# Two neighbouring rows per partition: wider expert-weight loads, an early second matrix, and a last norm in partition groups

## The reference

```python
x = _layernorm(DEEPNORM_ALPHA * x + mix, ln1_g, ln1_b)
# per token: top 4 of 32 experts, softmax over the selected logits
hgu = xb @ moe_w_gu[e] + moe_b_gu[e]          # (1024) x (1024, 2048)
gate, up = hgu[:, :D_EXPERT], hgu[:, D_EXPERT:]
gate = jnp.minimum(gate, 7.0); up = jnp.clip(up, -7.0, 7.0)
act = (up + 1.0) * gate * jax.nn.sigmoid(1.702 * gate)
out = act @ moe_w_down[e] + moe_b_down[e]     # (1024) x (1024, 1024)
y = sum over a token's experts of weight * out
x = _layernorm(DEEPNORM_ALPHA * x + y, ln2_g, ln2_b)
```

## Time and profile before

| | |
|---|---|
| median of three timed runs | 1255.13 us |
| the profiled execution | 1250.65 us, span 1248.7 us |
| TensorE busy | 1167.9 us (94%) |
| VectorE, ScalarE, GpSimd busy | 385.5, 278.4, 19.3 us |
| moved by DMA | 456.94 MB, mean 366 GB/s |
| loads of the first matrix from SyncE into `gu_w` | 252 of 1024 KB, and 4 early |
| loads of the second matrix | 256 of 512 KB |

### The profile page before, as it was taken

The page is one execution under the profiler, slowest core; times in us unless marked ns, Lnnn a source line. Parts: engine busy times, 40 slices in busy tenths (PEclk is TensorE's granted clock), DMA queues, the critical chain, the costliest instruction groups (busy, mean ns, idle before and its releaser), DMA issues.

```text
span 1248.7 us, 17368 instructions
## 1 busy us (share of the span) xinstructions
PE 1167.9 (94%) x6686; PEld 643.9 (52%) x6686; DVE 385.5 (31%) x719; ACT 278.4 (22%) x505; POOL 19.3 (2%) x39
## 2 busy tenths in 40 slices
PE   9999999999999999999999997999999999898995
PEld 8999879985434343444344442444343434343441
DVE  4888587753020202122203110211202020202025
ACT  5685454432111010101010110011111101010101
POOL 1000021000000000000000000000000000000000
PEclk9999999999999999998999998999999999999998
DMA  9745578887999999999999999999999999999994
GB/s 281 236 134 172 167 239 271 327 313 289 357 418 416 418 417 418 418 418 418 416 417 418 418 417 416 418 417 418 418 419 417 419 417 419 417 418 418 417 417 160
DMA packets 118351, 456.94 MB, mean 366 GB/s; under 512 B 10408, under 2 KB 49336, under 8 KB 85312
## 3 DMA queue, kind: packets, MB, share of 16 engines
q1 hardware_dynamic: 115728, 447.08, 90.3%
q0 software_dynamic: 2576, 9.21, 2.3%
HBM read 450.30 MB, written 5.95 MB: 365 GB/s over the span
## 4 chain that ended last, share of the span: by engine, by line
PE 73%; DMA 9%; SPq 7%; DVE 4%; issue 3%; ACT 2%; DVEq 0%; ACTq 0%
PE pool L957 25%; PE pool L878 15%; DMA gu_w<-in_moe_w_gu 8%; PE ub L838 6%; PE pool L607 5%; PE pool L608 4%; PE pool L609 4%; SPq L404 4%; PE ob L968 3%; SPq L399 3%; PE ub L968 2%; DMA dn_w<-in_w_in 1%; ACT arena L1204 1%; PE pool L894 1%; PE ob L907 1%
## 5 line engine op out<-in xcount | busy, mean ns | idle before, releaser
L957 PE MATMUL pool<-gu_w,arena 128*64 128x512 f32 x1920 | 425.2, 598 | 6.9 <-DMA gu_w<-in_moe_w_gu 6.9
L957 PEld LDWEIGHTS pool<-gu_w,arena 128*64 128x64 f32 x1920 | 138.4, 138 | 276.9 <-issue 247.2
L878 PE MATMUL pool<-dn_w,arena 128*64 128x512 f32 x1024 | 226.7, 595 | 20.3 <-ACT arena L1204 20.3
L1682 DVE TENSOR_SCALAR arena<-pool 128x512 f32<-128x512 f32 x31 | 21.4, 692 | 713.0 <-PE pool L957 708.1
L607 PE MATMUL pool<-xh,wh 128*128 128x264 f32 x568 | 164.4, 289 | 1.3 <-DVE xl L1254 0.6
L609 PE MATMUL pool<-xh,wl 128*128 128x264 f32 x568 | 161.4, 284 | 0.0
L878 PEld LDWEIGHTS pool<-dn_w,arena 128*64 128x64 f32 x1024 | 70.8, 137 | 156.0 <-issue 128.5
L1199 ACT ACTIVATE arena<-arena 128x512 f32<-128x512 f32 x32 | 20.2, 630 | 471.3 <-DVE arena L1682 471.3
L607 PEld LDWEIGHTS pool<-xh,wh 128*128 128x128 f32 x568 | 107.7, 190 | 8.0 <-issue 4.1
L608 PE MATMUL pool<-xl_most,wh 128*128 128x264 f32 x385 | 110.0, 286 | 0.0
L609 PEld LDWEIGHTS pool<-xh,wl 128*128 128x128 f32 x568 | 107.3, 189 | 0.0
(11 more groups left out here) (318 smaller groups left out, 783.3 us busy)
## 6 DMA issues: line engine op xcount, KB each, us to landing
gu_w<-in_moe_w_gu SPq DMA_DIRECT2D x252, 1024.0 KB, 17.6
dn_w<-in_moe_w_down SPq DMA_DIRECT2D x256, 512.0 KB, 15.4
dn_w<-in_w_in SPq DMA_DIRECT2D x24, 1024.0 KB, 5.8
dn_w<-in_w_branch SPq DMA_DIRECT2D x8, 1024.0 KB, 5.8
gu_w<-in_state_gla POOLq DMA_DIRECT2D x8, 512.0 KB, 6.6
out_gla_sample<-gu_w POOLq DMA_DIRECT2D x8, 512.0 KB, 5.0
dn_w<-in_w_o SPq DMA_DIRECT2D x4, 1024.0 KB, 7.6
arena<-in_moe_w_gu SPq DMA_DIRECT2D x4, 1024.0 KB, 9.0
```

The lines of the kernel that those rows point to most:

```text
L878: last = mm(DOWN[s * CAP:(s + 1) * CAP, :], act_t[:, k % 4, k // 4 * CAP:(k // 4 + 1) * CAP], dn_w[:, k, s * HF:(s + 1) * HF], start=(k == ...
L957: last = mm(out, xg[:, k, j * CAP:(j + 1) * CAP], gu_w[:, k, cols], start=False, stop=(k == NB - 1))
```

## The change

The rows of both expert matrices are dealt out differently. Two neighbouring rows of a matrix now go to one partition: partition p of blocks 2i and 2i+1 holds rows 256i + 2p and 256i + 2p + 1. One load fills two blocks (`load_two`, and `load_dn` for two at a time), with 16384 or 8192 contiguous bytes per partition; only the loads of expert 0's first matrix stay one block each. A load waits until both blocks have been used, and there are four semaphores in place of eight. The other operands follow: the gather reads every second column of `ytok` as its stationary operand, `turn_act` every second column of the activation, and the scale and bias come from copies `ln1_g2`, `ln1_b2` in the new order.

`early` now holds expert 1's second matrix, not half of its first; expert 1's first matrix is loaded whole into `gu_w`. In the last pair the residual rows are turned behind expert 31's first product instead of ahead of it. The decode rows' last norm is laid out as four partition groups of 8 rows and 256 columns, with the groups' means summed by a small product with a matrix of ones (`same`); the stores are one for the first group, four for the decode rows and two halves for the second group.

```diff
         rw_b = slot(9, 1800, NB * E).rearrange("p (k e) -> p k e", k=NB)
         ln2 = gu_w[:, 0, :].rearrange("p (a n) -> p a n", a=2)
-        EARLY = 4
-        early = [slot(i, 0, 2 * F) for i in (5, 3, 6, 0)]
+        early = [blocks(slot(i, 0, 2 * D), 2) for i in (5, 3, 6, 0)]
 
         yacc = blocks(slot(4), NB)
...
         stack = sb("stack", [P, E])
+        QD = D // 4
+        one = sb("one", [P, 8])
+        mvd, std, rsd = sb("mvd", [P, 2]), sb("std", [P, 6]), sb("rsd", [P, 3])
+        ln2d = Sg[:, 2:4, :].rearrange("p a n -> p (a n)").rearrange("p (a n) -> p a n", a=2)
+        yd = slot(0, 2 * D, QD)
...
 
-        FIN = [[ub[:, 0, :], ub[:, 1, :]], [ob[:, 0, :], ob[:, 1, :]], [GATE[0:DEC, :], UP[0:DEC, :]]]
+        FIN = [[ub[:, 0, :], ub[:, 1, :]], [ob[:, 0, :], ob[:, 1, :]]]
+        FIND, SUMD = GATE[:, 0:QD], UP[:, 0:2]
+        same = before
 
...
 
-                sp.dma_start(gu_w[:, k, :], w_gu[0, bass.ds(e, 1), k * P:(k + 1) * P, :]
-                             .rearrange("e p n -> (e p) n")).then_inc(gu_in[k], 16)
+                rows = w_gu[0, e, k // 2 * 2 * P:(k // 2 + 1) * 2 * P, :].rearrange("(p a) n -> p a n", a=2)
+                sp.dma_start(gu_w[:, k, :], rows[:, k % 2, :]).then_inc(gu_in[k // 2], 16)
+
+            def load_two(k, e):
+
+                sp.dma_start(gu_w[:, 2 * k:2 * k + 2, :], w_gu[0, bass.ds(e, 1), 2 * k * P:(2 * k + 2) * P, :]
+                             .rearrange("e (p a) n -> (e p) a n", a=2)).then_inc(gu_in[k], 16)
 
             def load_dn(k, e):
 
-                sp.dma_start(dn_w[:, k, :], w_down[0, bass.ds(e, 1), k * P:(k + 1) * P, :]
-                             .rearrange("e p n -> (e p) n")).then_inc(dn_in[k], 16)
-
-            def load_early(k):
-
-                sp.dma_start(early[k], w_gu[0, 1, k * P:(k + 1) * P, :]).then_inc(gu_in[EARLY + k], 16)
+                sp.dma_start(dn_w[:, 2 * k:2 * k + 2, :], w_down[0, bass.ds(e, 1), 2 * k * P:(2 * k + 2) * P, :]
+                             .rearrange("e (p a) n -> (e p) a n", a=2)).then_inc(dn_in[k], 16)
+
+            def load_early(i):
+
+                sp.dma_start(early[i], w_down[0, 1, 2 * i * P:(2 * i + 2) * P, :].rearrange("(p a) n -> p a n", a=2)
+                             ).then_inc(dn_in[i], 16)
 
             def load_x(half):
...
             for i in range(len(tiles) - 4, len(tiles)):
                 sp.wait_ge(w_lo, 2 * i + 2)
-                for k in (2 * (i % 4), 2 * (i % 4) + 1):
-                    load_dn(k, 0)
...
-                for k in range(NB):
-                    sp.wait_ge(gu_used, n * NB + k + 1 - NB)
-                    load_gu(k, e)
-                for k in range(NB):
-                    sp.wait_ge(dn_used, n * NB + k + 1 - NB)
+                for k in range(NB // 2):
+                    sp.wait_ge(gu_used, n * NB + 2 * k + 2 - NB)
+                    load_two(k, e)
+                for k in range(NB // 2):
+                    sp.wait_ge(dn_used, n * NB + 2 * k + 2 - NB)
                     load_dn(k, e)
 
             def body(it, pair):
                 load(it * 2 + 1, pair * 2 + 1)
...
-            for i in range(EARLY):
-                sp.wait_ge(gu_used, i + 1)
-                sp.dma_start(gu_w[:, i, :], w_gu[0, 1, (EARLY + i) * P:(EARLY + i + 1) * P, :]).then_inc(gu_in[i], 16)
-            for k in range(EARLY, NB):
-                sp.wait_ge(gu_used, k + 1)
-                load_gu(k, 2)
-            for i in range(EARLY):
-                sp.wait_ge(gu_used, NB + i + 1)
-                load_gu(i, 2)
             for e in (1, 2):
-                for k in range(NB):
-                    sp.wait_ge(dn_used, (e - 1) * NB + k + 1)
-                    load_dn(k, e)
+                for k in range(NB // 2):
+                    sp.wait_ge(gu_used, (e - 1) * NB + 2 * k + 2)
+                    load_two(k, e)
+            for k in range(NB // 2):
+                sp.wait_ge(dn_used, 2 * k + 2)
+                load_dn(k, 2)
 
             at = moe_loops(sp, body)
             load(at * 2 + 1, E - 1)
@@ -499,12 +507,17 @@
             for i, row in enumerate((ln2_g, ln2_b)):
                 sp.dma_start(ln2[:, i, :], row.partition_broadcast(P).rearrange("p a e -> p (a e)")).then_inc(ln2_in, 16)
 
-            for i, t in enumerate((2, 0, 1)):
-                first, rows = TILES[t]
-                sp.wait_ge(y2_done, i + 1)
-                dst = y_prompt[0, first:first + rows, :] if t < 2 else y_sample.rearrange("b s d -> (b s) d")
-                sp.dma_start(dst, y2[0:rows, t, :]).then_inc(stored, 16)
-            sp.wait_ge(stored, 16 * NT)
+            sp.wait_ge(y2_done, 1)
+            sp.dma_start(y_prompt[0, 0:P, :], y2[:, 0, :]).then_inc(stored, 16)
+            sp.wait_ge(dec_done, 1)
+            for j in range(4):
+                sp.dma_start(y_sample.rearrange("b s d -> (b s) d")[:, j * QD:(j + 1) * QD], yd[32 * j:32 * j + DEC, :]
+                             ).then_inc(stored, 16)
+            for s in range(2):
+                cols = slice(s * HF, (s + 1) * HF)
+                sp.wait_ge(y2_done, s + 2)
+                sp.dma_start(y_prompt[0, P:SEQ, cols], y2[:, 1, cols]).then_inc(stored, 16)
...
             for i in range(4):
                 pool.wait_ge(dst_out[i], 32)
+            for j in range(4):
+                for i, row in enumerate((ln2_g, ln2_b)):
+                    pool.dma_start(ln2d[32 * j:32 * j + DEC, i, :],
+                                   row[:, j * QD:(j + 1) * QD].partition_broadcast(DEC).rearrange("p a e -> p (a e)")
+                                   ).then_inc(ln2d_in, 16)
...
                         n = 4 * half + c
-                        last = mm(GATH[:, half, c * P:(c + 1) * P], ytok[0:rows, t, n * P:(n + 1) * P], pick[0:rows, t, :],
+                        last = mm(GATH[:, half, c * P:(c + 1) * P], ytok[0:rows, t, n // 2 * 2 * P + n % 2:(n // 2 + 1) * 2 * P:2],
+                                  pick[0:rows, t, :],
                                   start=(t == 2 and c == 0), stop=(t == 1), skip_group_check=True)
                 last.then_inc(then, 1)
...
                 for c in range(4):
-                    last = nc.tensor.transpose(ACTT[:, c * P:(c + 1) * P], act_s[:, c * P:(c + 1) * P], ident[:, :])
+                    last = nc.tensor.transpose(ACTT[:, c * P:(c + 1) * P],
+                                               act_s[:, c // 2 * 2 * P + c % 2:(c // 2 + 1) * 2 * P:2], ident[:, :])
                 last.then_inc(act_tr, 1)
 
...
                     for out, cols in quarters(GATE, UP):
                         last = mm(out, xg[:, k, 0:CAP], gu_w[:, k, cols], start=False, stop=(k == NB - 1))
                     last.then_inc(gu_used, 1)
 
-                for i in range(NB):
-                    k = (i + EARLY) % NB
-                    if i == EARLY:
...
+                    if k == 4:
                         pe.wait_ge(oh_ready, 2)
                         for out, cols in quarters(GATE1, UP1):
                             mm(out, oh[:, :], b3[:, cols], start=False, stop=False)
...
-                    w = early[k] if k < EARLY else gu_w[:, k - EARLY, :]
+                    pe.wait_ge(gu_in[k // 2], 48)
                     for out, cols in quarters(GATE1, UP1):
-                        last = mm(out, xg[:, k, CAP:2 * CAP], w[:, cols], start=(i == 0), stop=(i == NB - 1))
+                        last = mm(out, xg[:, k, CAP:2 * CAP], gu_w[:, k, cols], start=(k == 0), stop=(k == NB - 1))
                     last.then_inc(gu_used, 1)
-                down(0)
+                down(0, dn_w, 32)
                 turn_act(1)
                 pe.wait_ge(picked, 2)
                 pe.wait_ge(scat_read, 1)
...
                     elif final:
+                        for t, s in ((0, 0), (0, 1), (1, 1), (1, 0)):
+                            if (t, s) == (1, 0):
+                                pe.wait_ge(swt_last, 1)
+                            final_rows(FIN[t][s], s, t * P, P)
                         pe.wait_ge(gclip, n + 1)
                         pe.wait_ge(gu_read, n + 2)
-                        for s in range(2):
-                            final_rows(FIN[2][s], s, SEQ, DEC)
+                        for c in range(NB):
+                            row, col = c // 2 * 32, c % 2 * P
+                            mm(FIND[row:row + DEC, col:col + P], yacc[:, c, SEQ:T], ident[:, :],
+                               start=(c % 2 == 0), stop=False, skip_group_check=True)
...
-                                pe.wait_ge(swt_last, 1)
-                            final_rows(FIN[t][s], s, t * P, P)
 
             first_pair()
             body(moe_loops(pe, body, amid), PAIRS - 1, final=True)
 
-            pe.wait_ge(eo_last, 2)
-            for t in (2, 0, 1):
-                first, rows = TILES[t]
+            for t in range(2):
                 for s in range(2):
-                    mm(FIN[t][s], swT[:, first:first + rows], eo[:, s * HF:(s + 1) * HF],
```

(86 more changed lines are left out.)

53 lines of the change are left out of this document (32 added, 21 removed).

## The result

The changed kernel took 1240.78 us (median of four runs, 1237.88 to 1241.82) against 1255.06 us in the same comparison; the ratio is 0.990, with a 95% interval of 0.9881 to 0.9918. In a second comparison it took 1240.33 us against 1251.21, again a ratio of 0.9902 (0.9885 to 0.9919). The prediction was 1244.6 us with a range of 1240.5 to 1256. The direction is right; the time lies 3.8 us under the forecast and only 0.3 us inside the lower end of the range, and the median of the second comparison lies 0.2 us outside it. The profiled execution took 1237.88 us, span 1236.2, and is the fastest of the four; the one before took 1250.65, span 1248.7.

A forecast was written before the change was run, and what follows sets the result against it. Two close limits: the expert weight stream, costing TensorE 10.7 us of late waits, and TensorE's own work. 8.7 + 1.6 + 0.3 - 0.1 = 10.5 us off 1250.65 gives 1240.1, plus 4.5: 1244.6 us, range 1240.5 to 1256.

The forecast's parts named there:

- The stream: Expert weight loads: larger pieces save 8.3 ns fixed cost each, taking an expert from 30.16 to 29.62 us.
- B: Rival on weight loads: 16384-byte pieces gain nothing over 8192, giving 1250.1 us; chance 0.14.
- C: Rival on weight loads: two rows are not joined into one piece, rates stay, giving 1256.5 us; chance 0.07.
- a later start: Start of the weight stream at expert 2: refilling slots in pairs moves it from 346.9 to 349 us.
- The waits: TensorE's waits for late weights in the last four pairs: 10.7 us fall to 2 (0 to 4), gaining 8.7.
- near tie: At expert 31, its first matrix lands near 1202 us and TensorE wants the last two blocks at 1203.4.
- Strided weights: Gather and activation's turn reading every second float as stationary operand: taken as zero, bounds 0 to 5.3 us a pair.
- rival D: Strided stationary loads in gather and turn cost more, deciding from 0.7 us a pair, up to 1325 us; chance 0.13.
- The beginning: Experts 0 to 2: no wait for expert 1's weights, expert 2 still begins at 343.44 us; zero, bounds 0 and 2.
- The end: After expert 30: moved residual rows gain 1.6 us; final norm and stores gain 0.3, bounds -1 and +1.5.
- terms from T + 5.0 on: Final norm's DVE operations after the decode rows' products: together 9.1 us, ending DVE at T + 14.1.
- The sum: Whole kernel: 10.5 us gained, profiled execution 1240.1 us, median 4.5 us more at 1244.6.

The follow-up runs named there:

- e1: Changed kernel with every two-block load of both matrices issued as two loads, pieces of 8192 and 4096 bytes again; 1253.18 us, ratio 1.001.
- e2: Changed kernel with only the first matrix's two-block loads split again, 8192-byte pieces for both matrices; 1246.70 us, ratio 0.9954.
- f1: The changed kernel again, unaltered, as yardstick; 1240.33 us.
- f3: Changed kernel with VectorE writing the activation in the new row order, so its turn reads contiguously; the gather still reads every second column; 1239.80 us.
- e3: Changed kernel with contiguous stationary operands for gather and activation's turn, residual rows' channels in another order (timing only); 1237.63 us, ratio 0.9884.
- f2: Changed kernel with the middle block two pairs of experts later (MIDDLE = 7); 1244.98 us, ratio 0.9951.
- g1: Kernel before the change with seven tiny products (14 TensorE instructions) ahead of its first projection; 1250.88 us, ratio 0.9997.
- e4: Changed kernel with the residual prompt rows turned between experts 30 and 31 again; 1244.41 us, ratio 0.9932.

## Why the prediction was right

**The stream, right in mechanism and size.** The fixed cost of a piece was read as 8.3 ns and a mean of 424.8 GB/s follows from 29.62 us an expert; the plateau is 426, so 29.5. e1 and e2 take the pieces away and the gain goes with them, which ends rivals B (16384 bytes gain nothing over 8192: e2 is that kernel, 1246.7, where B said 1250.1) and C (not joined: e1, 1253.2, where C said 1256.5, and the page of the kernel after lists 124 loads of 2048 KB, in a stream of 426 GB/s). The step from 418 to 426 GB/s is 0.58 us an expert over 64 pieces an engine, 9 ns each. The single 16384-byte piece was estimated at 614.3 ns, and the trace's median is 614. By the Trainium skill, "DMA: Bandwidth & Descriptors", section "Why small descriptors are slow (HBM only)", the fixed overhead of a packet is about 3 cycles; at the 850 MHz of its section "Specifications" that is an estimate of 3.5 ns. The measurement decides, and it is more than twice that.

Summed by the stream: it ended at 1227.0 before and at 1214.0 after, 13.0 us earlier. Some 370 MB at 417.7 and at 426.2 GB/s differ by 17.7 us; the dip at the middle block takes 5.0 back (4.1 us of idle in the stretch with 248 GB/s, the rest beside it). The prediction had 16 us, 2 us for a later start and 4 for dips, one in the middle and one at the half, and so an end at 1212 in place of 1221, 9 us earlier; both ends lay too early, by 2 and by 6 us. The start cost nothing in sum: the stream pauses longer at 345 us (259 against 375 GB/s), but it had moved more in the twenty microseconds before (430 and 419 against 351 and 331 GB/s). At the half there was no dip.

**The waits.** Forecast 2 us of 10.7 left (0 to 4). In the kernel after the starts of the second products stay 28.90 and 28.43 us apart in turn up to 1184.39, so nothing is lost there, and 0.23 us behind it. In f1 the three distances ahead of the last are 28.80, 30.00 and 29.05 us, 2.1 us lost. The view of waits sums more (2.1 and 0.2 us after, 5.9 and 1.5 in f1; 24.8 and 6.9 before for the 10.7), since a load that waits beside a running product costs nothing. It is the near tie that the prediction names, and it falls to either side from run to run.

**Strided weights: the step that failed.** "I take zero", says the prediction. The gather takes 6.43 us against 6.13 (in the chain; the earlier trace rows is the timeline's 6.20), 0.30 us or 6 ns on each of 48, and the turn's loads 199 ns against 140. Most of the 59 ns is covered by what runs beside it: f3 takes the stride from the turn alone and its pair is 0.05 us shorter. e1, which has the strides without the longer issue gaps, runs its pairs in 28.83 + 28.36 = 57.19 us, 0.36 over the kernel before; the gaps make it 57.33. From 421.60 to 1184.39, outside the middle block and the half, 13 distances between second products are 28.90 us instead of 28.50 and 11 are 28.43 instead of 28.33: together 6.3 us of TensorE's time. That is inside the bounds given (0 to 5.3 us a pair) and under the 0.7 from which rival D decides; D is ruled out by e3, whose median is 3 us better and not 80. By the Trainium skill, "SBUF — State Buffer", section "Specifications", two hits per 16-byte line keep full bandwidth, and every second float has two. By that rule the price is zero; the traces show a small one, and they decide.

**TensorE's chain, and why the miss didn't show.** From the second product at 421.25 to that at 1195.38 the kernel before took 774.13 us; from 421.60 to 1184.39 the kernel after took 762.79, 11.34 less. The waits for weights give -10.7, where 8.7 were forecast. The unforeseen rest is the slower pair, +6.3, and the two places where TensorE's pattern breaks: the middle block (605.64 - 563.41 = 42.23 to 40.65) and the half (39.06 to 33.66), together 81.29 to 74.31, -7.0; in f1 they are 42.34 and 31.70, 74.04. Most of it is the second stall, gone. The shorter middle block is no work of the change, since f1, the same kernel, has 42.34; there the same products run longer: the granted clock over them is 0.83 and then 0.50 (579.2 to 581.7 us and to 584.2), where it is still 1.00 in the kernel after (576.7 to 579.2). In the kernel after and in f1:

```profile
578.14 1.05 PE L961 MATMUL ob<-arena 32*128 32x264 f32 x4
579.03 1.05 PE L961 MATMUL ub<-arena 32*128 32x264 f32 x4
...
580.58 1.70 PE L961 MATMUL ob<-arena 32*128 32x264 f32 x4
582.07 1.96 PE L961 MATMUL ub<-arena 32*128 32x264 f32 x4
```

So +6.3 and -7.0 cancel. With the stall still there TensorE's own work ends the kernel: f2 is that case, no pair of it waits for weights, and it is 4.6 us slower. In the kernel before the stall was free, as g1 shows, since there the stream sets the end. The sum held partly by luck: the stream's term was right, and two terms of TensorE's were missing that happened to be alike.

The same two traces of one kernel show how much an execution alone can move. In f1 the last second product starts 4.23 us later than in the kernel after's trace: 2.4 us of it stand ahead of expert 0 (291.47 against 289.04), where the change does nothing, 1.7 in the middle block, 2.1 in waits for weights, and -2.0 at the half.

**The beginning.** TensorE waited for no block of expert 1, as forecast, and began expert 2 at 343.19 us in the timeline, before at 343.44. But it had begun expert 0 at 289.04, before at 289.92. From there to expert 2 it took 54.15 us instead of 53.52: the 0.6 us more are the strided loads again (a gather of the first pair takes 3.23 us instead of 3.08 in the chain, the long one 6.43 instead of 6.13).

**The end.** From the start of expert 30's second product to T, the end of the last product, 35.11 us passed before (1195.38 to 1230.49) and 33.82 after (1184.39 to 1218.21), 0.23 us of it a wait that is counted above: 1.5 us, forecast 1.6. In e4 the old place cost 3.6 to 4.1 us by the medians, more than that; in its trace 2.5 us are a product that ran partly at the lower clock. The prediction's terms from T + 5.0 on add up to 9.6 us and not to the 9.1 that it writes, so its own rows give T + 14.6 for the end of DVE; T + 14.1 came near what was measured through this slip. In the tail DVE ends at T + 14.0 (forecast T + 14.1), the stores are issued from T + 13.4 and the last one begins near T + 15.3 (forecast T + 15.4), and the span ends at T + 18.0, before T + 18.2: 0.2 us for 0.3.

**The sum.** 11.34 + 1.3 + 0.2 - 0.35, the last for 421.60 against 421.25, are 12.5 us, the difference of the spans; forecast 10.5. The 2 us are the waits, 1.8 us fewer than forecast in that run, and small remainders. The forecast of the time was 3.8 us too long: 2.2 us of it in the profiled execution (1240.1 against 1237.88), and 1.6 us because the median was put 4.5 us over the profiled execution, as in the kernel before, and lay 2.9 over it. The medians differ by 14.3 us in the first comparison and 10.9 in the second: the kernel after was alike in both, the kernel before was not.

## What to carry to other kernels

Two piece sizes in one stream give the fixed cost of a piece, and with it the rate of a third size that no row shows; here that came out within 0.3% for the mean (424.8 against 426). Where a stream and an engine end nearly together, price an edit on both sides: a saving counts only on the side that ends last, while a cost of half a microsecond a pair on the other side eats it unseen. Work that can be moved belongs into the last wait ahead of a product that sets the end. A new stall at a loop's edge should be tried with the program shifted before it is put down to the edit. And two traces of the same kernel should be compared part by part before a difference of one or two microseconds in one part is put down to a change.
